# Odd-frequency transforms folded to half their matmuls, attention operands split and stacked at another time, and modulation rows transposed, in a two-block kernel

## The chip, the cores and the metric

One NeuronCore of a Trainium2 chip runs the whole program. The metric is device time in microseconds (us), the median of the runs of a kernel. The engines are named as in the profile: PE (TensorE, with PEld for its weight loads), DVE (VectorE), ACT (ScalarE), POOL (GpSimd) and SP (SyncE, which here only issues DMAs). Each runs its own instructions in order, and they wait for each other on semaphores.

## The reference

Two transformer-like blocks run one after the other on 512 tokens of width 1024, in float32. The change touches the first block only, in its mixing part:

```
hl = rmsnorm(xl, norm1_g) * (1.0 + sc1_l) + sh1_l          # sc, sh: rows of silu(c) @ ada_w + ada_b
aq, ak, av, bq, bk, bv, pool, hy = split_cols(hl @ w_in)   # and the same of 256 context tokens
a_l = diff_attention(...)            # 4 heads x 2 maps, 768 keys, softmax, p0 - lam * p1, @ v
b_l = neighbourhood_attention(...)
p_l = pool_mix(pool, ...)
h_l = hyena_mix(hy, ...)

def bidir_long_conv(u, h_fwd, h_bwd, d_skip):              # called twice by hyena_mix
    k = concatenate([h_fwd, zeros_like(h_fwd[:1]), h_bwd[:0:-1]])
    y = irfft(rfft(u, n=2 * L) * rfft(k), n=2 * L)[:L]     # L = 512
    return y + u * d_skip

z = x1 * bidir_long_conv(v, filt[:, 0, 0], filt[:, 0, 1], d_skip[0])
h = x2 * bidir_long_conv(z, filt[:, 1, 0], filt[:, 1, 1], d_skip[1])
xl = xl + g1_l * (concatenate([a_l, b_l, p_l, h_l]) @ w_out)
```

After it come a mixture of 16 experts, and a second block with attention, a state-space branch and gates. The filters `filt` come from a small network on 512 time steps.

## The kernel before, in words

The program is written engine by engine, each with its instructions in the order of the code; nothing reorders them. PSUM is used as four slots of two banks. A table of units (`units_of_block_one`, line 135) says in which order PE fills them and which engine, ACT or DVE, empties each; a unit reuses the slot of the unit four places earlier and waits for its release. `filled` waits until PE has filled a unit, `read` until it has been emptied. Weights come as slabs of 2 MB into a ring of three slots, issued by SP in the order of `SLABS_FIRST`.

The long convolutions are done as matmuls with cosine and sine tables at 512 odd frequencies, with the phase (2f+1) t pi/1024, in four tiles of 128 frequencies (QT = 4).

- Filter spectra, `spectra(f)`, four units of 2 x 4 matmuls (cosine and sine, four tiles of time, 512 columns for two filters of 256 channels). ACT copies each to `spec`. Two units stand ahead of the norm sums `n1`, `nf`, two after `ada(4)`.
- `transposes(o)` brings the gated input u to time-major form, ACT copies it to `hy_tm`; `forward(o, f)` (`fwd`, four units of 8 matmuls with 256 columns); DVE multiplies with the spectrum in `spectrum(o, f)` (four ops) into `hy_Y`; `inverse(o, c)` (`inv`, two units of 8 matmuls with 512 columns); DVE scales and gates the result (`gated`, `gate_out`).
- The first convolution (o = 0) runs after the projections. The second one (o = 1) is spread through the first attention ("a"), at the steps of `CONV_AT`: step 1 transposes, 3, 6, 9 and 11 forward, 15 and 16 inverse. A step i of this attention is, on PE, the transposes `t` of step i-1's probabilities, two score units of step i+1, a convolution unit where there is one, and the product with the values, `o`, of step i-1. On DVE it is `row_max`, `combine`, `row_max`, the convolution's ops, `output`.

The modulation rows, `ada(j)`, are twelve products of silu(c) with a slab of `ada_w`, in four row groups of PSUM; ACT copies the rows and `ada_tr(j)` sums the groups and brings them to columns in one go: four matmuls with the selection matrix `ada_sel` of two columns. DVE adds the bias.

Queries and keys of attention a are split in a rounded high part and a low rest (`q_hi_a`, `q_lo_a`, `k_hi_a`, `k_lo_a`). Both lie in hT, the normalised input, and so are written when the last projection (bv) has read hT. SP then stacks them four times over the partitions with 32 small DMAs (`stack`), the queries to `q_4` and the keys to `k_4` in the ring. The first scores wait for all 32. The tables for the forward transform are loaded twice to `fwd`, since preparations of the state-space part (`prep_pb`, `prep_ca`, `prep_ed` on DVE, stored by POOL) use the place in between; SP issues the second load when those stores have landed.

## Time and profile before

| what | value |
|---|---|
| runs | 1355.93, 1349.57, 1352.05 us |
| median | 1352.05 us |
| span of the profiled execution | 1354.0 us |
| instructions | 17167 |
| PE busy, weight loads | 1250.7 us (92%), 914.0 us (67%) |
| DVE, ACT, POOL busy | 843.6 (62%), 586.8 (43%), 132.3 us (10%) |
| mean granted clock of TensorE | 0.959 of full speed |

The profile is of one execution, and its times are in us from the start of the span. A row of the timeline gives start, length, engine, line of the code, operation, output and inputs, the shapes, and how many instructions were merged; brackets at the end give the engine's idle time just before it and who ended it. A float32 matmul shows as two records. Ends of matmuls are modelled, so that lengths of neighbouring groups overlap by a tenth or two.

### The profile page before, as it was taken

The numbers are of one execution on the slowest core, as the hardware profiler recorded it, in microseconds if no ns is written. First come the engines' busy times: TensorE is split into PE (matmuls) and PEld (weight loads), VectorE is DVE, ScalarE is ACT, GpSimd is POOL, SyncE is SP. The second block draws the span as 40 slices with busy tenths as digits, with TensorE's granted clock in tenths as the row PEclk, the third lists the DMA queues.
The fourth block names the chain that finished last, engine by engine and source line by source line (L and its number), as shares of the span: only waits on it lengthen the run. The fifth ranks groups of instructions, "written<-read, shape, count | busy, mean of one in ns | idle before, by whom it ended". The sixth has DMA issues, their size and how long they took to land.

```text
span 1354.0 us, 17167 instructions
## 1 busy us (share of the span) xinstructions
PE 1250.7 (92%) x6556; PEld 914.0 (67%) x6556; DVE 843.6 (62%) x1262; ACT 586.8 (43%) x777; POOL 132.3 (10%) x126
## 2 busy tenths in 40 slices
PE   6999999988889898699999999989999898989996
PEld 1444465766768776588888888658877777765774
DVE  3259878636866636678888898664227555724543
ACT  0540001214545553367877777533334343334322
POOL 2000101000015000112111212210000000000000
PEclk8999999998999999799999999999999999898998
DMA  8726546475040034489999999761344455534301
GB/s 361 294 76 263 226 182 246 163 156 124 1 179 21 1 129 186 143 315 397 411 409 399 408 405 406 284 245 62 114 140 132 149 172 151 166 116 180 125 0 62
DMA packets 52823, 270.69 MB, mean 200 GB/s; under 512 B 15031, under 2 KB 22071, under 8 KB 38040
## 3 DMA queue, kind: packets, MB, share of 16 engines
q1 hardware_dynamic: 38408, 210.04, 42.4%
q0 software_dynamic: 9744, 47.19, 9.5%
q10 hardware_dynamic: 4608, 12.58, 2.4%
q8 instruction: 43, 0.70, 0.2%
q14 instruction: 20, 0.16, 0.0%
HBM read 229.95 MB, written 36.70 MB: 197 GB/s over the span
## 4 chain that ended last, share of the span: by engine, by line
PE 77%; DVE 12%; ACT 4%; issue 3%; DMA 2%; POOL 1%; SPq 0%; DVEq 0%; ACTq 0%; POOLq 0%
PE PS L2736 27%; PE PS L3154 7%; PE PS L3155 7%; PE PS L3156 7%; PE PS L3068 3%; PE PS L3380 3%; PE PS L3381 3%; PE PS L3382 3%; PE PS L3285 2%; PE PS L3286 2%; PE PS L3287 2%; PE PS L3022 1%; PE PS L3366 1%; PE PS L2753 1%; PE PS L3148 1%
## 5 line engine op out<-in xcount | busy, mean ns | idle before, releaser
L2736 PE MATMUL PS<-arena 128*128 128x64 f32 (+6 forms) x770 | 188.0, 410 | 24.2 <-DMA arena<-in_small_f_w 7.7
L1385 ACT ACTIVATE arena_r<-ring 128x2048 fp32r<-128x2048 f32 x100 | 185.8, 1910 | 10.4 <-ACT arena L1422 8.1
L2736 PEld LDWEIGHTS PS<-arena 128*128 128x128 f32 (+2 forms) x770 | 114.8, 197 | 89.4 <-issue 58.4
L2186 DVE TENSOR_TENSOR arena_r<-ring,arena_r 128x2048 fp32r<-128x2048 f32 x66 | 148.1, 2285 | 20.9 <-ACT arena_r L1385 20.8
L2736 PE MATMUL PS<-hT,ring 128*128 128x512 f32 (+1 forms) x304 | 119.2, 550 | 0.0
L3154 PE MATMUL PS<-arena_r,hT_r 128*128 128x512 f32 x272 | 112.7, 414 | 4.9 <-DVE hT_r L2369 4.9
L3380 PE MATMUL PS<-arena_r 128*128 128x512 f32 x256 | 105.7, 413 | 12.0 <-DVE ring_r L2595 6.9
L3155 PE MATMUL PS<-arena_r,hT_r 128*128 128x512 f32 x272 | 109.0, 401 | 0.0
L1200 ACT ACTIVATE arena<-PS 128x1024 f32<-128x1024 f32 (+2 forms) x31 | 28.5, 926 | 169.6 <-PE PS L2736 155.0
L3382 PE MATMUL PS<-arena_r,ring_r 128*128 128x512 f32 x256 | 101.8, 398 | 0.0
L2736 PEld LDWEIGHTS PS<-hT,ring 128*128 128x128 f32 x304 | 57.1, 190 | 59.0 <-issue 56.6
L2186 DVE TENSOR_TENSOR hT_r<-ring,arena_r 128x2048 fp32r<-128x2048 f32 x34 | 76.4, 2288 | 26.6 <-ACT arena_r L1385 26.3
L2595 DVE TENSOR_TENSOR ring_r<-ring,arena_r 128x1024 fp32r<-128x1024 f32 (+1 forms) x40 | 40.4, 1011 | 69.8 <-ACT arena_r L1542 69.2
L3381 PE MATMUL PS<-hT_r,arena_r 128*128 128x512 f32 x192 | 76.6, 399 | 0.0
L1875 DVE TENSOR_TENSOR arena<-arena 128x512 f32<-128x512 f32 (+2 forms) x104 | 71.9, 691 | 3.6
L3380 PEld LDWEIGHTS PS<-arena_r 128*128 128x128 f32 x256 | 49.4, 193 | 29.6 <-issue 7.5
L3154 PEld LDWEIGHTS PS<-arena_r,hT_r 128*128 128x128 f32 x272 | 52.1, 191 | 20.4 <-DVE hT_r L2369 5.5
L3155 PEld LDWEIGHTS PS<-arena_r,hT_r 128*128 128x128 f32 x272 | 52.4, 193 | 11.1
L2410 DVE TENSOR_TENSOR ring_r<-ring,arena_r 128x1024 fp32r<-128x1024 f32 x18 | 21.9, 1224 | 59.7 <-ACT arena_r L1482 59.7
L1542 ACT ACTIVATE arena_r<-ring 128x1024 fp32r<-128x1024 f32 (+1 forms) x40 | 35.4, 885 | 53.8 <-PE PS L3382 51.0
L3382 PEld LDWEIGHTS PS<-arena_r,ring_r 128*128 128x128 f32 x256 | 49.6, 194 | 11.8
L3156 PE MATMUL PS<-arena_r,hT_r 128*128 128x512 f32 x136 | 55.4, 407 | 0.0
(473 smaller groups left out, 2388.4 us busy)
## 6 DMA issues: line engine op xcount, KB each, us to landing
ring<-in_moe SPq DMA_DIRECT2D x51, 2048.0 KB, 10.3
ring<-in_slabs SPq DMA_DIRECT2D x27, 2048.0 KB, 11.2
ring<-in_slabs SPq DMA_DIRECT2D x9, 1024.0 KB, 5.7
y_rows<-arena ACTq DMA_DIRECT2D x16, 512.0 KB, 10.0
ssm_scratch<-arena POOLq DMA_DIRECT2D x4, 1152.0 KB, 6.6
arena<-ssm_scratch POOLq DMA_DIRECT2D x4, 1152.0 KB, 8.3
arena<-in_tab_fwd SPq DMA_DIRECT2D x2, 2048.0 KB, 15.6
ssm_scratch<-arena POOLq DMA_DIRECT2D x4, 1024.0 KB, 11.6
```

Source lines behind the costliest of these rows:

```text
L1385: nc.scalar.activation(rounded(moe_w_hi[n][:, cols]), ring[:, n, cols], ACT.Copy).then_inc(s_moe_hi[n], 1)
L1875: then(nc.vector.tensor_tensor(out, x, y, op))
L2186: nc.vector.tensor_tensor(rounded(moe_w_lo[n][:, cols]), ring[:, n, cols], as_float(moe_w_hi[n][:, cols]), ALU.subtract).then_inc(s_moe_lo ...
L2595: nc.vector.tensor_tensor(rounded(w), w, as_float(w_hi[:, n % 2, 0:w.shape[1]]), ALU.subtract).then_inc(s_w_lo, 1)
L2736: ins = nc.tensor.matmul(out, lhsT, rhs, start=(n == 0), stop=(n == len(pairs) - 1))
L3068: ins = nc.tensor.matmul(bank(key, c), rounded(w[:, k]), rounded(x[:, k]), start=(m == 0), stop=(m == 3 * KD - 1))
L3154: nc.tensor.matmul(out, rounded(x_hi), rounded(w_hi_), start=first, stop=False)
L3155: nc.tensor.matmul(out, rounded(x_lo), rounded(w_hi_), start=False, stop=False)
L3156: return nc.tensor.matmul(out, rounded(x_hi), rounded(w_lo_), start=False, stop=last)
L3380: nc.tensor.matmul(out, w_h, x_h, start=(k == 0), stop=False)
L3381: nc.tensor.matmul(out, w_h, x_l, start=False, stop=False)
L3382: ins = nc.tensor.matmul(out, w_l, x_h, start=False, stop=(k == last))
```

## The change

The cosine and the sine of frequency 511 - f differ from those of f only by a sign at the even or the odd time steps. So the changed kernel sorts time into even and odd steps (`evens_odds`, `split_time`, `time_of`), computes the transforms of both halves for 256 frequencies only (FT = 2 tiles), and gets the frequencies above by a sum and a difference. The inverse does it the other way round.

- `spectra(n)`: four units of 2 x 2 matmuls (even and odd half). ACT copies the odd half (`filter_odd`), DVE forms sum and difference (`filter_spectrum`).
- `forward(o, f)`: two units of 8 matmuls with 256 columns. ACT copies the odd half (`forward_odd`). DVE: `spectrum_products` (sum, difference, two products of 1024 elements) and `spectrum_sums` (two sums, and the sum and difference for the inverse). `CONV_AT` is now {1, 4, 8, 15}; in attention a the sums run one step after the products.
- `inverse(o, c)`: two units of 8 matmuls with 256 columns.
- The short convolutions read every second element and write sorted.
- The query's and key's high and low parts have places in the arena. The query is split before `ada(11)`, ahead of the short convolutions on DVE; the key after them. SP stacks the queries when bk_ctx is filled, the keys after `ada(11)`; the second unit of bv stands between forward and inverse. DVE's sums wait for the stacked high parts of the keys, ACT's odd copy for the stacked queries, since these are overwritten. `w_in` slab 2 is laid out so that its first half is free earlier, and the ring slots 1 and 2 of the `w_in` slabs are swapped.
- The second load of `fwd`, now 1 MB, is issued by ACT.
- `ada_tr(j)`: four transposes against the identity; DVE sums the four groups with a reduce and adds the bias in an op of its own.

```diff
-SECOND_CONV = [("u_tr", 1)] + [("fwd", 1, f) for f in range(QT)] + [("inv", 1, c) for c in range(2)]
-CONV_AT = {1: 0, 3: 1, 6: 2, 9: 3, 11: 4, 15: 5}
+FT = 2
+HALF = T // 2
+SECOND_CONV = [("u_tr", 1)] + [("fwd", 1, f) for f in range(FT)] + [("inv", 1, c) for c in range(2)]
+CONV_AT = {1: 0, 4: 1, 8: 2, 15: 3}
...
+            def forward_odd(o, f):
+
+                filled(act, ("fwd", o, f))
+                if o or f:
+
+                    act.wait_ge(s_spec, FT * o + f)
+                nc.scalar.activation(hy_V[:, 1].rearrange("p a b -> p (a b)"), bank(("fwd", o, f), 1), ACT.Copy).then_inc(s_odd, 1)
...
             act.wait_ge(s_out_pb, 32 * Q_SSM)
+            act.wait_ge(s_out_ed, 32 * Q_SSM)
+            act.dma_start(fwd, tab_d["fwd"]).then_inc(s_fwd_in, 16)
+            read(act, ("ak_ctx",))
+            nc.scalar.activation(rounded(k_hi_a), k_a, ACT.Copy).then_inc(s_qk_hi, 1)
             copy_unit(("bv", 0), v_b[:, 0:4].rearrange("p a b -> p (a b)"), both(("bv", 0)))
...
+            act.wait_ge(s_stack_q, 16 * 16)
+            for f in range(FT):
+                forward_odd(0, f)
...
-                nc.vector.tensor_tensor(mod[:, a:b], bank(key, 0)[:, 0:8].rearrange("p (a b) -> p a b", b=2),
-                                        V("ada_b", a, b)[:, :, None].broadcast_to([P, b - a, 2]),
-                                        ALU.add).then_inc(s_dve_read, 1)
+                of_groups = bank(key, 0).rearrange("p (m g r) -> p m r g", m=4, g=4)[:, :, 0:2]
+                nc.vector.tensor_reduce(mod[:, a:b], of_groups, AX_X, ALU.add).then_inc(s_dve_read, 1)
+                read(dve, key)
+                then(nc.vector.tensor_tensor(mod[:, a:b], mod[:, a:b], V("ada_b", a, b)[:, :, None].broadcast_to([P, b - a, 2]),
+                                             ALU.add))
...
-            def spectrum(o, f):
+            def spectrum_products(o, f):
...
+                dve.wait_ge(s_odd, 2 * FT + FT * o + f + 1)
+                then(nc.vector.tensor_tensor(flat[:, 0], bank(key, 0), flat[:, 1], ALU.add))
+                nc.vector.tensor_tensor(flat[:, 1], bank(key, 0), flat[:, 1], ALU.subtract).then_inc(s_dve_read, 1)
...
+                then(nc.vector.tensor_tensor(hy_M, hy_V, cos_f, ALU.mult))
+                then(nc.vector.tensor_tensor(hy_V, hy_V, sin_f, ALU.mult))
+
+            def spectrum_sums(o, f):
+
+                nc.vector.tensor_tensor(hy_M[:, :, 0], hy_M[:, :, 0], hy_V[:, :, 1], ALU.subtract).then_inc(s_dve, 1)
...
+                then(nc.vector.tensor_tensor(hy_M[:, :, 1], hy_M[:, :, 1], hy_V[:, :, 0], ALU.add))
+                if o == f == 0:
+                    dve.wait_ge(s_stack_k[0], 16 * 8)
+                elif f == 0:
+                    dve.wait_ge(s_stack_k[1], 16 * 8)
+                then(nc.vector.tensor_tensor(hy_Y[o][:, f, 0], hy_M[:, 0], hy_M[:, 1], ALU.add))
+                nc.vector.tensor_tensor(hy_Y[o][:, f, 1], hy_M[:, 0], hy_M[:, 1], ALU.subtract).then_inc(s_spec, 1)
...
-                    ins = products(bank(key, 0)[:, 2 * m:2 * m + 2], [(ada_row[:, P * m:P * m + P], ada_sel[:])])
+                    ins = nc.tensor.transpose(bank(key, 0)[:, P * m:P * m + P], ada_row[:, P * m:P * m + P], ident[:])
...
             transposes(0)
-            for f in range(QT):
+            for f in range(FT):
                 forward(0, f)
+            tokens("bv", w_bv, 0, [1])
             pe.wait_ge(s_inv_in, 16)
             for c in range(2):
                 inverse(0, c)
```

How the instructions move, at three places. First PE, from the last projections to the end of the first convolution. `ring,hT ... x32` and `x16` are bv's two units, `ident,arena 128x128 x8` the transposes of u, `arena 128x256` forward or (now) inverse, `arena 128x512` the inverse before. Before:

```order
L2736 MATMUL PS<-ring,hT 128x256 x32
L2736 MATMUL PS<-ada_sel,post 128x2 x4
L2736 MATMUL PS<-ring,hT 128x256 x16
L2938 MATMUL PS<-ident,arena 128x128 x8
L2736 MATMUL PS<-arena 128x256 x32
L2736 MATMUL PS<-arena 128x512 x16
```

Now:

```order
L2772 MATMUL PS<-ring,hT 128x256 x32
L2798 MATMUL PS<-ident,post 128x128 x4
L2973 MATMUL PS<-ident,arena 128x128 x8
L2772 MATMUL PS<-arena 128x256 x16
L2772 MATMUL PS<-ring,hT 128x256 x16
L2772 MATMUL PS<-arena 128x256 x16
```

The second bv unit has moved from before the transposes to between forward and inverse, and both transforms have half their columns.

Second, DVE in a step of attention a with a forward unit: `TENSOR_REDUCE stat` is `row_max`, the op on `hT` is `combine`, `TENSOR_SCALAR arena<-PS,stat` is `output`. Before:

```order
L2066 TENSOR_REDUCE stat<-PS 128x1
L2012 TENSOR_TENSOR arena<-PS,arena 128x512
L2014 TENSOR_TENSOR rstd<-PS,arena 128x512
L2017 TENSOR_TENSOR arena<-arena,rstd 128x256
L2018 TENSOR_TENSOR arena<-arena,rstd 128x256
L2084 TENSOR_SCALAR arena<-PS,stat 128x64
```

Now, from step 4 into step 5:

```order
L2040 TENSOR_TENSOR arena<-PS,arena 128x512
L2041 TENSOR_TENSOR arena<-PS,arena 128x512
L2044 TENSOR_TENSOR arena<-arena 128x1024
L2045 TENSOR_TENSOR arena<-arena 128x1024
L2117 TENSOR_SCALAR arena<-PS,stat 128x64
...
L2117 TENSOR_SCALAR arena<-PS,stat 128x64
L2049 TENSOR_TENSOR arena<-arena 128x2x256
L2051 TENSOR_TENSOR arena<-arena 128x2x256
L2056 TENSOR_TENSOR arena<-arena 128x512
L2057 TENSOR_TENSOR arena<-arena 128x512
```

The four ops of a unit have become eight, four in its own step before `output` and four in the next one after it. There are two such units instead of four. In the first convolution the eight ops stand in a row.

Third, ACT between the last modulation row and the first scores. `arena_r` outputs are the high parts. Now:

```order
L1239 ACTIVATE arena_r<-arena 128x1024
L1141 ACTIVATE post<-PS 128x512
L1244 ACTIVATE arena<-arena,vec 128x512 x6
L1248 DMA arena<-in_tab_fwd 128x2048
L1250 ACTIVATE arena_r<-arena 128x1536
L1203 ACTIVATE arena<-PS 128x1024 x2
L1170 ACTIVATE arena<-PS 128x512 x2
L1203 ACTIVATE arena<-PS 128x512
```

Before, the query's high part stood behind both bv copies, the key's behind the copy of the transposes, the two odd copies of line 1170 and the DMA did not exist here.

## Rows read from the trace of the kernel before

**Rows 1.** The page: busy time per engine, and the chain's shares by engine.
```profile
PE 1250.7 (92%) x6556; PEld 914.0 (67%) x6556; DVE 843.6 (62%) x1262; ACT 586.8 (43%) x777; POOL 132.3 (10%) x126
...
PE 77%; DVE 12%; ACT 4%; issue 3%; DMA 2%; POOL 1%; SPq 0%; DVEq 0%; ACTq 0%; POOLq 0%
```

**Rows 2.** Timeline of PE: filter spectra (two groups) and one modulation transpose.
```profile
44.91 15.68 PE L2736 MATMUL PS<-arena 128*128 128x512 f32 x32
...
71.53 14.00 PE L2736 MATMUL PS<-arena 128*128 128x512 f32 x32
85.36 0.95 PE L2736 MATMUL PS<-ada_sel,post 128*128 128x2 f32 x8
```

**Rows 3.** Timeline of ACT in the first stage: table load after squares, root, third spectrum.
```profile
54.27 1.28 ACT L1176 ACT_TABLE_LOAD   x1
...
66.58 0.27 ACT L1185 ACTIVATE root<-PS,of_rows 128x6 f32<-128x6 f32 x1 [0.46 <-PE PS L2736]
...
78.70 1.02 ACT L1165 ACTIVATE arena<-PS 128x1024 f32<-128x1024 f32 x1 [6.44 <-PE PS L2736]
```

**Rows 4.** Timeline of DVE: tenth modulation row, and the last short convolution.
```profile
244.73 0.17 DVE L1730 TENSOR_TENSOR mod<-PS,vec 128x8 f32<-128x8 f32 x1 [3.76 <-PE PS L2736]
...
263.00 0.75 DVE L1997 SCALAR_TENSOR_TENSOR arena<-arena,vec 128x512 f32<-128x512 f32 x1
```

**Rows 5.** Timeline of PE: transposes, forward, inverse, first scores.
```profile
275.21 1.04 PE L2938 MATMUL PS<-ident,arena 128*128 128x128 f32 x8
277.96 14.05 PE L2736 MATMUL PS<-arena 128*128 128x256 f32 x64 [1.72 <-ACT arena L1200]
294.47 15.67 PE L2736 MATMUL PS<-arena 128*128 128x512 f32 x32 [2.46 <-DVE arena L2018]
309.58 2.09 PE L2736 MATMUL PS<-ring_r 128*128 128x512 f32 x8
```

**Rows 6.** Timeline of ACT (a copy of 512), DVE (1024 from SBUF, 512 from PSUM).
```profile
275.41 0.60 ACT L1200 ACTIVATE arena<-PS 128x512 f32<-128x512 f32 x1 [6.72 <-PE PS L2736]
...
276.98 1.23 DVE L2042 TENSOR_TENSOR hT_r<-arena,hT_r 128x1024 fp32r<-128x1024 f32 x1 [8.42 <-ACT hT_r L1247]
...
281.69 0.69 DVE L2012 TENSOR_TENSOR arena<-PS,arena 128x512 f32<-128x512 f32 x1 [0.67 <-PE PS L2736]
```

**Rows 7.** Stacking DMAs; median landing of the 2 MB table; a window while stacking.
```profile
L808 SPq DMA_DIRECT2D ring_r<-hT_r x32: 594/602/1547, 277.0 to 300.9; - x32
...
arena<-in_tab_fwd SPq DMA_DIRECT2D x1, 2048.0 KB, 8.7
...
282.00:290.00 8.00, 8.00 (x39) 7.04 (x38) 5.26 (x11) 0.00 (x0) 0.00 (x0) 1.00 0.96 205
```

**Rows 8.** Timeline of PE and DVE in attention a, steps 3 to 16.
```profile
326.54 0.85 PE L3022 MATMUL PS<-ident,hT 128*128 128x128 f32 x6 [0.31 <-DVE hT L2076]
...
333.53 0.82 PE L3022 MATMUL PS<-ident,hT 128*128 128x128 f32 x6
...
336.08 1.02 DVE L2076 SCALAR_TENSOR_TENSOR hT<-hT,stat 128x768 f32<-128x768 f32 x1
...
337.24 0.85 PE L3022 MATMUL PS<-ident,hT 128*128 128x128 f32 x6 [0.37 <-DVE hT L2076]
...
341.19 0.82 PE L3022 MATMUL PS<-ident,hT 128*128 128x128 f32 x6
...
377.01 0.84 PE L3022 MATMUL PS<-ident,hT 128*128 128x128 f32 x6 [0.44 <-DVE hT L2076]
...
386.71 8.32 PE L2736 MATMUL PS<-arena 128*128 128x512 f32 x28
...
399.60 7.13 PE L2736 MATMUL PS<-arena 128*128 128x512 f32 x16
```

**Rows 9.** Windows (us): length, busy PE, PEld, DVE, ACT, POOL, clock, DMA share, GB/s.
```profile
294.00:298.00 4.00, 3.53 (x5) 1.57 (x6) 0.72 (x2) 0.00 (x0) 0.00 (x0) 0.63 1.04 224
...
345.00:360.00 15.00, 13.10 (x86) 11.22 (x85) 12.54 (x23) 8.03 (x15) 0.00 (x0) 1.00 0.00 1
```

More of the change, by code:

```diff
@@ L2948, in forward @@
                     pe.wait_ge(s_fwd_in, 32)
-                for cs in range(2):
-                    products(bank(key, 0)[:, HY * cs:HY * cs + HY],
-                             [(fwd[:, cs, t, P * f:P * f + P], hy_tm[:, t]) for t in range(QT)], last=(cs == 1))
+                for odd in range(2):
+                    for cs in range(2):
+                        products(bank(key, odd)[:, HY * cs:HY * cs + HY],
+                                 [(fwd[:, cs, t, P * f:P * f + P], hy_tm[:, t]) for t in range(2 * odd, 2 * odd + 2)],
+                                 last=(odd == cs == 1))
             def inverse(o, c):
@@ L2955, in inverse @@
                 start_unit(key)
-                pe.wait_ge(s_spec, QT * (o + 1))
-                products(bank(key, 0), [(hy_Y[:, f, cs, P * c:P * c + P], inv[:, cs, f])
-                                        for cs in range(2) for f in range(QT)], last=True)
+                pe.wait_ge(s_spec, FT * (o + 1))
+                for odd in range(2):
+                    times_ = slice(HALF * odd, HALF * odd + HALF)
+                    products(bank(key, 0)[:, times_], [(hy_Y[o][:, f, odd, cs, P * c:P * c + P], inv[:, cs, f, times_])
+                                                       for cs in range(2) for f in range(FT)], last=(odd == 1))
             def second_conv(n):
@@ L2966, in _ @@
             transposes(0)
-            for f in range(QT):
+            for f in range(FT):
                 forward(0, f)
+            tokens("bv", w_bv, 0, [1])
             pe.wait_ge(s_inv_in, 16)
@@ L3535, in slabs_of @@
         elif name == "w_in":
-            out.append(k_major(a["w_in"][0][:, 512 * j:512 * j + 512], 512))
+            w, cols = a["w_in"][0][:, 512 * j:512 * j + 512], 256 if j == 2 else 512
+            out.append(np.concatenate([k_major(w[:, at_:at_ + cols], cols) for at_ in range(0, 512, cols)], axis=1))
         elif name == "w_out":
```

202 lines of the change are left out of this document (102 added, 100 removed).

## The prediction

> **What bounds the kernel now.** I read the page's busy shares first: TensorE (PE) is busy 92% of the span, VectorE (DVE) 62%, ScalarE (ACT) 43%, and the chain of work that ended last lies 77% on PE, 12% on DVE [rows 1]. So PE's matmuls set the time, except where PE waits. Then I read PE's timeline over the first 400 us, since the change ends there. In it the reader should see long groups without idle brackets (every matmul removed there is time gained, as long as nothing else comes last), and a few groups with brackets, which name who comes last. Four places matter: the filter transforms at 44.91 and 71.53 [rows 2], the first convolution at 277.96 to 309.58 [rows 5], the first attention at 326.54 to 377.01 [rows 8], and the inverse transforms at 386.71 and 399.60 [rows 8].
>
> A float32 matmul shows as two records, and its time goes by columns: 32 records of 512 columns take 14.00 us (0.44 each) [rows 2], 64 of 256 take 14.05 (0.22 each) [rows 5]. A transpose is one record: six take 0.82 [rows 8].
>
> **First stage, -15.0 us.** The filter spectra fall from 32 to 16 matmuls of 512 columns, 14.0 us less on PE. Half of them stand ahead of the norm sums. There ACT ends its squares at 54.27 and computes the norm's root at 66.58 [rows 3]; between, it waits for PE. After the change PE's first spectra end near 52.8 (44.91, less 0.9 for the faster row transposes ahead, plus half of 15.68 and the 0.9 us that the slow clock costs beyond that half), so ACT comes last: table load 1.28 and a short root 0.1, two copies of 0.5 (the new odd halves, which are 512 wide), a copy of 0.8, and PE's small matmuls until the root, 1.6. From 53.9 (squares 0.4 earlier) that gives the root at 58.7, 7.8 us earlier. The second pair saves its full 7.0 [rows 2]: the normalised h is ready in time, since ACT's copy of the third spectrum, for which it waited 6.44 us ahead of h [rows 3], now stands behind h. Each of the modulation transposes saves about 0.4: eight records of 2 columns take 0.95 [rows 2], four transposes at 0.11 each take 0.5. One of them lies here: 7.8 + 7.0 + 0.4, less 0.2 for rounding, 15.0. What comes next late here would be a slab for PE; the DMA engines are idle most of the time from 56 on and the forward table is 1 MB less, so I cost loads at nothing.
>
> **From there to the first transform, -2.6 and -7.1.** Seven more row transposes (5 to 11) lie before it: 7 x 0.37 = 2.6. The second bv product, 32 records of 256 columns or 7.1 us by the price above, moves behind the forward transforms. PE would so reach the transposes of u at 275.2 - 15.0 - 2.6 - 7.1 = 250.6. Is DVE ready? It is the engine with most to do here. Its preparation chain starts after two more sums per filter spectrum (4 x 1.35 us), 14.1 us earlier than before; but it waits for PE twice on the way, last at 244.73 for 3.76 us [rows 4], and that wait ties it to PE again: -17.0 there, -16.8 after the extra op. Then 9.0 for the last preparation, the query low part now ahead of the convolution (1.23, [rows 6]), and 8.8 for twelve short convolutions, the last of which starts at 263.00 [rows 4]. It is done at 246.9, 3.7 us before PE. These twelve now read every second element. The bound above is twice their time, 8.8 us more, of which 5.1 would reach PE; below it is nothing, as the op's form stays. I take nothing. The modulation's extra reduce and add (0.25 us, 12 times) is in those figures.
>
> **First convolution, -5.2.** Before, from the transposes at 275.21 to the scores at 309.58: 34.4 us. After, step by step from 250.6. Transposes and ACT's copy 2.4: PE starts forward at 253.0. One forward unit still has 8 matmuls of 256, 3.45 us, but there are two. DVE sees it 0.2 later, at 256.7, and first ACT copies the odd half (0.6, as the 0.60 row of [rows 6]). Then DVE has eight ops where it had four [rows 6]: two on PSUM at 0.69, two products of 1024 elements at 1.23, and four of 512 at 0.69, with 0.04 between, 6.7 us where it was 2.2. ACT's second odd copy waits until all that is done, as it overwrites an operand, so the second unit runs wholly behind: 256.7 + 2 x (0.65 + 6.75) = 271.5. PE has its second forward unit and bv (to 267.2) as cover and then idles 4.3 us. Then the inverses, half the columns: 7.0, plus 1.7 for the slow clock after an idle stretch, which the same place shows now (15.68 for a 14.0 group [rows 5], clock 0.63 [rows 9]). End 280.3, scores 0.6 earlier as before, 279.7: 29.1 us, bv among them. Sum so far: 15.0 + 2.6 + 7.1 + 5.2 = **-29.9**.
>
> **The copies between.** The stacking of queries and keys takes 32 transfers of 128 or 192 KB, 5.2 MB, at 205 GB/s while the DMA engines are 0.96 busy [rows 7]. They had ended well before the scores. Now SP waits for the query split (236) and the bk_ctx products, and queued behind that wait stand only these copies. Sum of DMA work ahead of the key high copies' end, one after the other: queries 2.1 MB 10.5 us, prep stores 4, forward table 1 MB at half of 8.7 us [rows 7], key high 1.6 MB 7.9. From 236.1 that is 262.9; DVE needs them at its seventh op, about 262.5. I put +0.4. The low copies end near 271, wanted first at 280. ACT, which now issues the forward load, waits for the prep stores until at most 245; behind it in its queue is the bv copy, for which PE is ready at 250.4 only.
>
> From the trace alone the copies load the engines to 0.96. The Trainium skill, page "Trainium Kernel Development and Optimization", section Key Constraints, says that DMAs of the SP, ACT and POOL queues run on the same 16 engines and interleave, so the new queue buys only issue time. By that rule the forward table, issued at 245 beside the copies, may land at 255 and not at 250, and the sum would be +2 where a free queue would leave it at nothing; no row yet shows both at once.
>
> **First attention, +3.2.** Here a step without a convolution unit takes 3.95 us (337.24 to 341.19), one with a forward unit 6.99 (326.54 to 333.53), and ten steps with four units 50.5 (to 377.01) [rows 8]: a unit costs 2.9 over a base of 3.9, since PE sets such a step and DVE's 2.2 us hide in it. The change drops two units, and the tempting sum is -5.8. But DVE itself has 3.5 of the 3.9 us to do (a combination of 1.02 [rows 8], two row maxima of nearly as much, small ones), and a unit now brings it 6.7 us: 4.0 in its own step, 2.8 in the next. I follow it: t=0 at the step's transposes, unit filled at 5.9, odd copy to 6.6, products to 10.5, output, maximum and combination to 13.0, next transposes at 13.1 (now 10.7); the sums then hold the following ones to 19.3 (now 14.7); the step behind is 3.7. Four steps 22.9 where the base has 15.6: 7.3 per unit, 14.7 for two, against 11.5 for four now.
>
> **Inverses of the second convolution, -7.0.** PE sets both: the groups at 386.71 (with twelve small records) and at 399.60 have no idle ahead of what follows [rows 8], and each loses half of 7.0. What comes next in the second, the exponential's table load and DVE's maxima, also moves up.
>
> Sum: -29.9 + 0.4 + 3.2 - 7.0 = **-33.3**. Nothing later changes, and the expert stage, where DMA is full, starts earlier as a whole. The profiled execution has a span of 1354.0, so 1320.7; the median of the runs shown is 1352.05, 2 us less, and I forecast 1352.05 - 33.3 = 1319.
>
> **Rivals.**
> 1. DVE's extra work hides in attention as it does now: 2 units at 2.9, so 8.9 better, 1310. For it: the units stand four steps apart. Against: DVE has 0.4 us free per step.
> 2. PE's clock. Its idle stretches grow (4.3 us before the inverses, about 2 us in attention beside the waits for DVE). A gap of 2.5 us sufficed for 0.63 of the clock at 294 to 298, while from 345 to 360, with gaps below 1 us, it is 1.00 [rows 9]. Each fall costs 1.7 us where PE decides; two to five of them: 1322 to 1328.
> 3. Copies or table late: the interleaving above, +2 to +6: 1321 to 1325.
> 4. The first stage gives half, because a slab load or h comes last after all: 1326.
> 5. Slower than before: attention falls to the half clock and stays there, since its PE work (0.8 of transposes, 1.2 of scores and 1.5 of values) then takes 6 to 6.5 us and each step some 2.3 more; 16 steps, 37 us, for 1356. It decides from the point where the loss passes 33 us, which needs nearly all steps. Against it: 1.00 throughout the waits of now.
> 6. The change does not halve: the count in the order and the equal price per column exclude it but for 1%.
>
> **Chances.** Forecast (1315 to 1322) 0.50; rival 1 0.13; rival 2 0.16; rival 3 0.11; rival 4 0.06; rival 5 0.02; the last 0.02 for the sixth and what I don't see. Leaving out 0.2 at the most, the range is 1309 to 1327. A difference within 0.5%, 6.8 us, can't be told from no change here: faster 0.96, same 0.02, slower 0.02.
>
> **What would show it.** Pool products at about 71 on PE, not 86; transposes of u near 251 and not waiting for DVE; 4 us idle on PE before the inverse, released by DVE; transposes of attention 6 us apart twice after each unit; scores of the first attention at 280. Wrong would be: PE waiting for the stacked copies, steps of 3.9 behind a unit, or a first stage that moves by less than 12 us.

## The result, and the profile after

The changed kernel takes 1332.05 us (median of four runs, 1328.5 to 1342.4); the runs of the kernel before beside it give a ratio of 0.9847 (95% interval 0.9812 to 0.9883). Measured once more it is 1339.58 us and 0.9896 (0.9845 to 0.9946). So it is faster, by 16 to 20 us between the medians. I had forecast 1319, with a range from 1309 to 1327: the sign is right and the size is not.

The page of the profiled execution, with a span of 1332.2 us (before 1354.0): busy times, and the chain by engine.

```profile
PE 1220.0 (92%) x6412; PEld 899.1 (67%) x6412; DVE 862.2 (65%) x1282; ACT 588.6 (44%) x781; POOL 129.2 (10%) x126
...
PE 74%; DVE 13%; ACT 5%; DMA 3%; issue 3%; SPq 2%; POOL 1%; DVEq 0%; ACTq 0%; POOLq 0%
```

Against [rows 1] PE has 31 us less to do and DVE 19 more, and the chain has moved a little from PE to DVE. The span is only 22 us shorter. Where the rest went is read from PE's timeline. These are the groups that answer to [rows 2] and [rows 5], then the row of DVE that the prediction named as a danger:

```profile
45.79 7.03 PE L2772 MATMUL PS<-arena 128*128 128x512 f32 x16
...
62.80 2.91 PE L2772 MATMUL PS<-arena,ones 128*128 128x512 f32 x4
65.64 3.38 PE L2789 MATMUL PS<-ring,arena 128*32 128x512 f32 x16
68.94 7.13 PE L2772 MATMUL PS<-arena 128*128 128x512 f32 x16
75.92 0.60 PE L2798 MATMUL PS<-ident,post 128*128 128x128 f32 x4
76.35 6.17 PE L2893 MATMUL PS<-hT,ring 128*128 128x512 f32 x14
...
255.43 1.04 PE L2973 MATMUL PS<-ident,arena 128*128 128x128 f32 x8
257.69 7.14 PE L2772 MATMUL PS<-arena 128*128 128x256 f32 x32 [1.22 <-ACT arena L1203]
277.07 8.71 PE L2772 MATMUL PS<-arena 128*128 128x256 f32 x32 [5.33 <-DVE arena L2057]
285.43 1.88 PE L2772 MATMUL PS<-ring_r 128*128 128x512 f32 x8
```

```profile
268.00 0.69 DVE L2056 TENSOR_TENSOR arena<-arena 128x512 f32<-128x512 f32 x1 [0.53 <-DMA ring_r<-arena_r]
```

The counted work came out: both spectra groups are 7.0, a row transpose 0.60, the forward group 7.1, PE stands 5.3 us ahead of the inverse and is released by DVE. The two groups between them (62.80 and 65.64) are the diagonal sums and `ada(4)`; they took 1.53 and 1.92 us before, with the same work. In attention a (`t` groups of steps 4 to 8 and 10 to 12, which answer to [rows 8]):

```profile
305.81 0.82 PE L3064 MATMUL PS<-ident,hT 128*128 128x128 f32 x6
...
312.58 0.83 PE L3064 MATMUL PS<-ident,hT 128*128 128x128 f32 x6
...
318.84 1.51 PE L3064 MATMUL PS<-ident,hT 128*128 128x128 f32 x6 [0.66 <-DVE hT L2109]
...
324.80 1.51 PE L3064 MATMUL PS<-ident,hT 128*128 128x128 f32 x6 [0.57 <-DVE hT L2109]
...
329.48 0.85 PE L3064 MATMUL PS<-ident,hT 128*128 128x128 f32 x6 [0.26 <-DVE hT L2109]
...
342.74 1.51 PE L3064 MATMUL PS<-ident,hT 128*128 128x128 f32 x6 [0.66 <-DVE hT L2109]
...
348.70 1.51 PE L3064 MATMUL PS<-ident,hT 128*128 128x128 f32 x6 [0.58 <-DVE hT L2109]
...
355.03 1.25 PE L3064 MATMUL PS<-ident,hT 128*128 128x128 f32 x6 [1.27 <-DVE hT L2109]
```

Six transposes take 0.82 to 0.85 us, but 1.51 in steps 6 and 7 and in steps 10 and 11, where the units stand in steps 4 and 8. The windows say why: length, busy PE, PEld, DVE, ACT, POOL, then the granted clock. Steps 3 to 13, after and before:

```profile
301.80:359.50 57.70, 46.76 (x253) 40.06 (x253) 47.70 (x77) 28.88 (x53) 2.35 (x1) 0.79 0.09 33
```

```profile
326.50:377.00 50.50, 44.05 (x284) 37.98 (x285) 41.51 (x77) 27.75 (x51) 3.00 (x1) 1.00 0.04 9
```

There are 31 fewer matmul records, and PE is busy 2.7 us longer, since TensorE was granted 0.79 of its clock on average (at times the lower of its two levels, 1.2 GHz, where before it had the upper one, 2.4 GHz, throughout).

### The profile page after: what moved, and what is told of

Its sections match the earlier page's. It is cut to its first block, busy times and chain, and to the rows that moved or that the text cites. A ratio compares the mean times of both kernels' runs of the same rounds, so it can differ in the third digit from the quotient of the medians.

```text
span 1332.2 us, 16908 instructions
## 1 busy us (share of the span) xinstructions
PE 1220.0 (92%) x6412; PEld 899.1 (67%) x6412; DVE 862.2 (65%) x1282; ACT 588.6 (44%) x781; POOL 129.2 (10%) x126
## 4 chain that ended last, share of the span: by engine, by line
PE 74%; DVE 13%; ACT 5%; DMA 3%; issue 3%; SPq 2%; POOL 1%; DVEq 0%; ACTq 0%; POOLq 0%
PE PS L2772 21%; PE PS L3196 7%; PE PS L3197 7%; PE PS L3198 7%; PE PS L3110 3%; PE PS L3422 3%; PE PS L3423 3%; PE PS L3424 3%; PE PS L3328 2%; PE PS L3327 2%; PE PS L3329 2%; PE PS L3064 2%; PE PS L3408 1%; SPq L804 1%; PE PS L2789 1%
## 5 line engine op out<-in xcount | busy, mean ns | idle before, releaser
L2772 PE MATMUL PS<-arena 128*128 128x64 f32 (+6 forms) x674 | 150.1, 390 | 30.0 <-DMA arena<-in_small_f_w 7.6
L2772 PEld LDWEIGHTS PS<-arena 128*128 128x128 f32 (+2 forms) x674 | 100.2, 205 | 73.9 <-issue 40.5
L2223 DVE TENSOR_TENSOR hT_r<-ring,arena_r 128x2048 fp32r<-128x2048 f32 x34 | 76.4, 2288 | 26.9 <-ACT arena_r L1394 26.2
L3422 PEld LDWEIGHTS PS<-arena_r 128*128 128x128 f32 x256 | 49.2, 192 | 30.9 <-issue 9.7
L3424 PEld LDWEIGHTS PS<-arena_r,ring_r 128*128 128x128 f32 x256 | 49.2, 192 | 11.6
## 6 DMA issues: line engine op xcount, KB each, us to landing
ssm_scratch<-arena POOLq DMA_DIRECT2D x4, 1024.0 KB, 10.9
```

Source lines behind the costliest of these rows:

```text
L2223: nc.vector.tensor_tensor(rounded(moe_w_lo[n][:, cols]), ring[:, n, cols], as_float(moe_w_hi[n][:, cols]), ALU.subtract).then_inc(s_moe_lo ...
L2772: ins = nc.tensor.matmul(out, lhsT, rhs, start=(n == 0), stop=(n == len(pairs) - 1))
L3422: nc.tensor.matmul(out, w_h, x_h, start=(k == 0), stop=False)
L3424: ins = nc.tensor.matmul(out, w_l, x_h, start=False, stop=(k == last))
```

## The experiments

Each starts from the changed kernel, unless it says otherwise. To compare stages rather than medians I use distances on PE's timeline: first filter spectrum to pool products ("first stage"), pool products to transposes of u, from there to the scores ("convolution"), the t groups of steps 3 and 13 ("ten steps"), and step 13 to the first t of attention b ("the end"). In the first traces they were, before, 41.3, 189.04, 34.4, 50.5 and 29.6; after 30.6, 179.08, 30.0, 57.7 and 22.7.

**Both kernels once more.**

> The changed kernel once more, untouched, for a second trace. If the half-clock spells are a property of the program (my theory), they stand at the same places again: 62 to 69 behind the norm sums (ada(4) near 3.4 us, n1d near 2.9), behind both forward units of the first attention (transposes of 1.5 us instead of 0.85), and steps of 6.8, 6.3, 6.0, 4.7 and 7.0, 6.3, 6.0, 6.3. If they are chance (rival), at least one place reads 1.00 with ada(4) at 1.9. The spells near 424 and 444 in the second attention and at the third filter layer (1.7 us) I take as open: this trace tells whether they recur. Time 1332, ratio to the kernel before 0.985.

> The kernel before once more, untouched, for a second trace of it. Three traces of the new form show a mean granted clock of 0.83 to 0.86 from 300 to 375 (before: 0.96 over the first attention). If the spells come with the change, this trace again shows the clock near 1.00 between the third step and the inverses, and the ten steps with four units take 50.5 us. If they are chance, it shows half-clock transposes (1.5 us) there too, and ten steps of 52 or more. Open, since the runs of the new form differ in it: the third filter layer takes 7.1, 11.8 or 14.0 us; here it took 12.3 and I can't say which it will be. Time 1352 to 1356.

The changed kernel: first stage 30.1 with the diagonal sums at 2.91 and `ada(4)` at 3.44, pool products to u 179.08 again, convolution 29.6, steps of 6.77, 6.26, 5.96, 4.67 and 7.00, 6.26, 5.96, 6.34, 5.18. The first eight are those of the first trace to 0.02 us; the last, step 12, took 4.49 there. The kernel before (1354.42 us, ratio 0.9973, 0.9943 to 1.0004): 41.3, 189.04, 34.4, 50.5, and a granted clock of 1.00 over the ten steps. So the spells (stretches at the lower clock) in the first stage and behind the units come with the change. Not all do. The end took 27.6 in this trace of the changed kernel and 22.7 in the first, and 31.7 against 29.6 before; from the first t of attention b to the end of the span it was 947.4 and 948.9 before, 950.0 and 951.7 after, and 948.2 on average over twelve kernels below that change nothing there (940.7 to 953.8). The spells near 424 and 444 of the first trace belong to that scatter.

The third filter layer (`f3`) is a lottery of its own. It took 7.13 us here and 14.02 in the first trace, for the same sixteen records:

```profile
20.48 7.13 PE L2772 MATMUL PS<-arena 64*128 64x512 f32 x16 [0.72 <-ACT arena L1146]
```

```profile
20.24 14.02 PE L2772 MATMUL PS<-arena 64*128 64x512 f32 x16 [0.72 <-ACT arena L1146]
```

Both traces show a granted clock of 1.00 from 20 to 36 us, though the group of 14.02 us runs at half the pace. Up to 4 of the 7 us are left when the first spectrum starts (41.8 against 45.8; before 44.9 twice).

**The first stage.** PE's norm sums wait for ACT's squares after the change. Two kernels filled that wait. The first moves the third filter spectrum (PE's part is shown; ACT's and DVE's moved likewise):

```diff
             spectra(0)
             spectra(1)
+            spectra(2)
...
             ada(4)
-            spectra(2)
             spectra(3)
```

> The changed kernel with the third filter spectrum moved ahead of the norm sums, on PE, ACT and DVE. PE then has 3.5 us of dense products while ACT finishes its squares, and the norm sums run in one piece as they did before the change. Clock theory: no half clock between 62 and 69, n1d 1.5 and ada(4) 1.9 us, pool products start at 71.5 instead of 76.35, so 5 us less (3.3 of clock, 1.7 of waiting for squares), time near 1327. Rival (the squares and DVE's new sums alone set the stage, the clock is chance): the root comes 1.5 to 3.5 later, the spell stays, and pool products start between 75 and 77, no change in time.

The second adds four products of 128x512 in a bank that nobody reads:

```diff
+            banks_free(pe, ("nf",))
             for k in range(KD):
+                if k >= 4:
+                    nc.tensor.matmul(bank(("nf",), 1), ident[:], even_odd[:, 0, 0].rearrange("p a b -> p (a b)"), start=True, stop=True)
                 pe.wait_ge(s_sq, 2 * k + 2)
```

> The changed kernel with four products of 512 columns that nobody reads, one ahead of each of the last four waits for ACT's squares in the norm sums; PE does 1.75 us more work there, in time that it waits. Clock theory: n1d 1.5 and ada(4) 1.9 us, pool products start at 73 to 74 instead of 76.35, though PE does more. Rival (no clock effect, or the work that matters is elsewhere): pool products at 76.3 to 78, n1d and ada(4) slow as before.

With the third spectrum ahead the spell was gone in this trace, as expected, and the gain was not 5 but 1.9 us (first stage 28.7; median 1335.59, ratio 0.9851, 0.9772 to 0.9930, no different from the changed kernel):

```profile
62.11 1.53 PE L2772 MATMUL PS<-arena,ones 128*128 128x512 f32 x4
63.57 1.92 PE L2789 MATMUL PS<-ring,arena 128*32 128x512 f32 x16
...
72.35 4.96 PE L2893 MATMUL PS<-hT,ring 128*128 128x512 f32 x11 [2.79 <-issue]
```

The pool products now stand four units behind the diagonal sums and so reuse their PSUM slot, which DVE holds until h is scaled; PE waited 2.79 us for it. I had counted work and not slots. The filling products failed: first stage 35.5 us, 5 longer (median 1338.82, ratio 0.9892, 0.9857 to 0.9927). The rows explain the length. Eight norm sums (128x32 tiles) take 1.08 us when they stand together and two of them take 1.05 beside a full-width product, so these tiles run side by side only with one another:

```profile
52.82 1.08 PE L2850 MATMUL PS<-arena,ones 128*32 128x512 f32 x8
...
54.27 1.12 PE L2847 MATMUL PS<-arena,ident 128*128 128x512 f32 x2
55.32 1.05 PE L2850 MATMUL PS<-arena,ones 128*32 128x512 f32 x2
```

The spell came all the same: PE did not wait between the first spectrum and the diagonal sums, and these took 2.91 again, with a granted clock of 1.00 up to 68 us and 0.50 from 70 to 72. So the waits for the squares are not needed for the spell in this stage, and the clock theory of this run failed.

**Attention a: who holds a step.** The query of attention b was split in step 11, its high part on ACT, its low part on POOL. In the trace of the changed kernel a DVE op on one column took 1.88 us beside that POOL op, 0.22 elsewhere:

```profile
351.47 2.35 POOL L1002 TENSOR_TENSOR hT_r<-arena,hT_r 128x1024 fp32r<-128x1024 f32 x1 [108.19 <-ACT hT_r L1304]
351.77 0.15 DVE L2106 RECIPROCAL stat<-stat 128x2 f32<-128x2 f32 x1
351.96 1.88 DVE L2107 SCALAR_TENSOR_TENSOR stat<-stat,lam 128x1 f32<-128x1 f32 x1
```

```diff
             nc.scalar.activation(lam[:, 2:4], lam[:, 0:2], ACT.Exp).then_inc(s_lam_e, 1)
+            act.wait_ge(s_spec, FT)
+            read(act, ("bk_ctx",))
+            nc.scalar.activation(rounded(q_hi_b), q_b.rearrange("p j (i c) -> p j i c", c=256),
+                                 ACT.Copy).then_inc(s_qk_hi, 1)
...
-                if i == 9:
```

> The changed kernel with one edit: the query of the second attention is split at the start of the first inverse transform, where ACT and DVE are idle, and no longer at step 10 of the first attention. Theory: the 1.88 us for a DVE op on one column beside POOL's low part (0.22 elsewhere) is DVE held until POOL ends, so it goes, and so do ACT's 1.04 ahead of the copy of the transposes: the step that took 6.33 takes about 4.2, time 2 us less, near 1330. Rival (the long op has another cause, the step is slow by the half clock): a step of 5.9 or more stays and the time with it. A second check: POOL's op in its new place lies beside DVE at rest and costs nothing there; scores stay near 285.4.

The step fell from 6.33 to 5.18 (the transposes behind it still at 1.49), the ten steps from 57.7 to 55.7, and the median was 1327.01 (ratio 0.9807, 0.9745 to 0.9868). The direction is as expected, but the step is not at 4.2, since the half clock stayed. Nor is all of the 2.0 the query's: 0.7 of it lies in step 7, which took 3.95 and not 4.68 because the clock was up again earlier, long before the place of the query's op.

**How much of it is the clock.** Score products that nobody reads fill PE's waits: first only the last two lines of the diff, in steps 5 and 9, then all of it, on top of the early query split.

> The changed kernel with eight score products that nobody reads ahead of the value products in steps 5 and 9, where PE waits 2.2 us for DVE's output: PE is busy there and does 2 us more work. Clock theory: the transposes after that wait take 0.85 and not 1.5 us in steps 6, 7, 10 and 11, the steps behind become 4.0 instead of 4.7, and step 4 to step 12 takes 46.5 to 48 us instead of 49.2. Rival (DVE alone sets these steps; the half clock hides behind it): step 4 to step 12 at 49.2 or more, whatever the clock does.

```diff
+            def fill(key, times):
+                for _ in range(times):
+                    nc.tensor.matmul(bank(key, 1), rounded(q_4[:, 0, 0:P]), rounded(k_4[:, 0, 0:T]), start=True, stop=True)
...
+                        if a == "a" and i in (5, 6, 9, 10, 12, 13):
+                            fill(("a", "o", i - 1), {5: 3, 6: 7, 9: 3, 10: 7}.get(i, 3))
...
+                        if a == "a" and i in (4, 8):
+                            fill(("a", "o", i), 8)
```

> The kernel with the early query split, and score products that nobody reads wherever PE waits for DVE in the first attention: eight ahead of the value products of steps 5 and 9, three to seven ahead of the transposes of steps 6, 7, 10, 11, 13 and 14. Clock theory: with no gaps PE keeps the full clock, all transposes take 0.85 us, and from step 3 to step 13 the time is what the prediction gave without any fall, 53.7 us (55.7 in the run with the early query split alone, 57.7 in the changed kernel), and from there to the second attention 22.7 instead of 25.0. So 3 to 4 us less than that run. Rival (the half clock hides behind DVE all along): 55 to 56 and 25 stay.

With steps 5 and 9 alone filled (1330.23 us, 0.9816, 0.9788 to 0.9843), steps 4 to 12 took 49.2 as before. The transposes of step 6 were back at 0.85 us and the steps took 6.26 and 5.96 as ever; the half clock came one step later and the fourth step was 4.68. There the rival was right: steps 5 and 6 are DVE's, at either clock. It is the steps after them that the clock lengthens. With all waits filled and the query moved (1332.03, 0.9846, 0.9804 to 0.9889), steps 3 to 13 took 3.96, 6.75, 6.17, 5.96, 4.04, 6.70, 6.18, 5.96, 4.04 and 4.40, 54.2 in all, where the prediction had 53.7 (the median does not show it: it is 5 us above that of `q_split_early`, with intervals that overlap):

```profile
301.60:355.80 54.20, 47.87 (x293) 38.47 (x293) 46.67 (x78) 27.91 (x52) 0.00 (x0) 1.00 0.10 35
```

The 3.5 us between 57.7 and 54.2 divide so. In steps 3 to 10, ahead of the query's op, 1.1 went, which is the clock's. Steps 11 and 12 took 10.8 together in the changed kernel, 9.8 with the query moved and 8.4 with the waits filled too. So the clock has about 2.5 and the query's split about 1.0, when they are taken away in this order. But the end was 24.6 and not 22.7. In step 13 POOL's other low part started 0.04 us ahead of the combination:

```profile
358.28 3.50 POOL L1005 TENSOR_TENSOR arena_r<-arena,arena_r 128x1536 fp32r<-128x1536 f32 x1 [78.10 <-ACT arena_r L1308]
358.32 4.28 DVE L2109 SCALAR_TENSOR_TENSOR hT<-hT,stat 128x768 f32<-128x768 f32 x1
```

**Whether POOL holds DVE.** The edit: `pool.wait_ge(s_prob, n)` ahead of that POOL op, so that it starts behind the combination of step 13.

> Four edits together: the third filter spectrum ahead of the norm sums with the pool products ahead of the fifth row transposes; the early query split; the products that nobody reads in PE's waits of the first attention; and POOL's low part of the second attention's keys starts only when DVE's combination of step 13 is done. In the run with the fills, POOL started 0.04 us ahead of that combination and DVE's op took 4.28 us instead of 1.02. Theory (a DVE op that reads two tensors from SBUF waits until POOL is done): the combination takes 1.02 again, POOL is through before the next one, step 13 takes 5.3 instead of 6.9, and from step 13 to the second attention 23 instead of 24.6. Pool products 27 us behind the first spectrum, steps 3 to 13 at 54.2. Time 1320 to 1325, ratio 0.977. Rival (the long op has another cause): step 13 or 14 still takes 6 to 7.

The count of 13 was one too low (step 13's combination is the fourteenth), so the wait did nothing: POOL started 0.04 us ahead of the op once more, which took 4.27, and step 13 took 6.85. As a test of the cause this run is void; as a time it gave 1331.55 (0.9809, 0.9790 to 0.9827). With a count of 14 and nothing else changed against `fill_more`:

> The kernel with the early query split and the filling products, and one edit more: POOL's low part of the keys waits for the fourteenth combination, that of step 13 (with a count of thirteen it had not waited at all). Theory (a DVE op that reads two tensors from SBUF stands until POOL's op is done): POOL starts when the combination ends, the combination takes 1.02 and not 4.28 us, the step from the thirteenth to the fourteenth transposes takes 5.3 instead of 6.86, unless the next op with two inputs comes while POOL still works (3.5 us), which would then hold step 14. From step 13 to the second attention 22.5 to 23.1 instead of 24.6. Rival (the long op has another cause): 6.8 and 24.6 stay.

```profile
353.79 1.02 DVE L2110 SCALAR_TENSOR_TENSOR hT<-hT,stat 128x768 f32<-128x768 f32 x1
...
354.95 3.51 POOL L1006 TENSOR_TENSOR arena_r<-arena,arena_r 128x1536 fp32r<-128x1536 f32 x1 [79.06 <-DVE hT L2110]
```

The same op takes 1.02, the step 5.38, the end 22.8 (the prediction had 22.6), and the median is 1327.19 (0.9784, 0.9757 to 0.9811). That settles it: a DVE op that reads two tensors from SBUF, started while POOL's tensor_tensor runs, stands until POOL is done. DVE's row maximum, which reads PSUM, and its reciprocal, with one input, ran beside POOL at their usual 0.95 and 0.16. The Trainium skill, page "GPSIMD Engine Reference", section Specifications, says that GpSimd shares its SBUF interfaces with VectorE and contends with instructions that have two SBUF inputs; the traces agree, with 1.66 and 3.26 us for one instruction, and the prediction had not drawn on it. Nor had it seen that the trace of the kernel before holds such a pair, at the end of the filter network; this op takes 0.67 elsewhere:

```profile
33.98 2.35 POOL L973 TENSOR_TENSOR arena<-arena 128x1024 f32<-128x1024 f32 x1 [1.07 <-DVEq L1751]
34.00 2.89 DVE L1755 TENSOR_TENSOR arena<-arena 128x512 f32<-128x512 f32 x1
```

**Where the units stand.**

> The changed kernel with the second forward unit at step 6 of the first attention and not at 8. Theory (a unit costs what DVE has left over after it, because its eight ops come at the end of the unit's own step): DVE's sums of the first unit then stand in step 5, and its catching up in step 6 lies beside PE's second unit: steps of 6.8, 6.3, 6.8, 6.3, 6.0, 4.7 and then 4.0, so 44.5 us from step 4 to step 12 instead of 49.2, time 1328 to 1331. Rival (the clock sets these steps, and two units so near each other pull it down for longer): 48 to 50 us, with transposes of 1.5 in steps 5 to 9 throughout, and no gain.

```diff
-CONV_AT = {1: 0, 4: 1, 8: 2, 15: 3}
+CONV_AT = {1: 0, 4: 1, 6: 2, 15: 3}
```

The ten steps took 56.3, 1.4 less and not 4.7; steps 4 to 12 took 48.7, within the rival's 48 to 50. The median was 1332.43 (0.9831, 0.9806 to 0.9857), no different from the changed kernel. Steps 6 and 7 took 7.41 and 7.54. DVE stood 1.62 us for the unit and its odd copy, and PE's scores then waited for the unit's PSUM slot, its value products for DVE's output behind the products:

```profile
324.45 0.59 ACT L1170 ACTIVATE arena<-PS 128x512 f32<-128x512 f32 x1
325.14 0.69 DVE L2040 TENSOR_TENSOR arena<-PS,arena 128x512 f32<-128x512 f32 x1 [1.62 <-PE PS L3064]
...
326.61 0.62 PE L2772 MATMUL PS<-ring_r 128*128 128x512 f32 x2 [1.19 <-DVE arena L2041]
...
329.45 2.52 PE L2772 MATMUL PS<-arena 128*128 128x64 f32 x12 [2.22 <-DVE arena L2117]
```

I took the odd copy's place, behind an exponential on ACT, for the cause. The next two kernels carry the third spectrum, with a new place for one modulation row so that the pool products reuse another slot, the early query split and this `CONV_AT`:

```diff
             spectra(3)
-            ada_tr(4)
...
             pair(("pool",), w, 0, first_time=True)
+            ada_tr(4)
```

> Three edits on the changed kernel: the third filter spectrum ahead of the norm sums, now with the pool products ahead of the modulation's fifth transposes (they waited 2.8 us for a PSUM slot in the run before); the query split of the second attention at the first inverse; the second forward unit at step 6. Theory: 4.5 us in the first stage (pool products 26 us behind the first spectrum instead of 30.5), 2.4 from the query, 4.7 from the unit, so 11 to 12 less than the changed kernel, 1321 to 1326. Rival (spells of half clock fall where the waits now stand and give part of it back): 1327 to 1332.

and on top of it, on ACT:

```diff
+                        if (a, i, c) == ("a", 7, 1):
+                            forward_odd(1, 1)
                         act.wait_ge(s_max, j + 1)
...
-                        elif key[0] == "fwd":
+                        elif key == ("fwd", 1, 0):
```

> The kernel with the three edits, and ACT's odd copy of the second unit ahead of the exponential of score 7 and no longer behind it. In the run before, DVE stood still for 1.9 us at step 6 for that copy, and step 6 and 7 took 8.95 and 6.54. Theory: the copy ends at once when the forward products end, DVE's products start 0.8 to 1.4 us earlier, PE's scores don't wait for the unit's slot, and step 3 to step 13 falls from 55.65 to 54.0 to 54.8. Rival: the copy now holds the exponential, which the combination waits for, and nothing is won (55.5 or more).

`three_edits`: 1328.05 (0.9796, 0.9771 to 0.9820), where its rival had it and not the theory, first stage 26.9, ten steps 55.65, the two steps 8.95 and 6.54. With the odd copy first: 1325.79 (0.9792, 0.9754 to 0.9830), ten steps 55.6, the two steps 8.94 and 6.53. The copy's place on ACT changed nothing, because in both traces PE's forward products themselves were slow (6.50 us where 4.90 is usual); placed first, the copy only waited 2.39 us for them. My theory of the odd copy fell; the neighbouring units cost about what they cost apart.

**One part undone, and the clean version.**

```diff
-                    ins = nc.tensor.transpose(bank(key, 0)[:, P * m:P * m + P], ada_row[:, P * m:P * m + P], ident[:])
+                    ins = products(bank(key, 0)[:, 2 * m:2 * m + 2], [(ada_row[:, P * m:P * m + P], ada_sel[:])])
```

> One part of the change undone: the modulation's row sums again by four products with two columns, and DVE's one op instead of two. By the prediction's price of 0.37 to 0.4 us each, seven of them stand between the pool products and the transposes of u: 181.7 to 181.9 us between these two instead of 179.08, which four traces of the changed form agree on to 0.01. Rival (DVE's own chain sets that stretch, and the second op on DVE costs what PE gains): 179.1 stays.

From pool products (74.38) to transposes of u (256.42): 182.04, 2.96 more. The row transposes are worth 0.42 each. (It ran once, in 1341.56 us, which says nothing by itself.)

> Three edits without any filling products: third filter spectrum ahead of the norm sums with the pool products ahead of the row transposes, early query split, POOL's key part behind the combination of step 13. Theory: no DVE op is held by POOL; the half clock stays where PE waits (steps 6, 7, 10, 11), so steps 3 to 13 take 55.5 to 56.5 and step 13 to the second attention 22.7 to 25. Pool products 27 to 28.5 us behind the first spectrum: two of three traces with this order had the slow n1d of 2.91 us all the same, so I expect 28.5 here. Time 1322 to 1328.

This one gives 1325.84 (0.9797, 0.9776 to 0.9818), with no unread products. First stage 25.3 us, with both groups at the full clock, ten steps 55.0, the end 23.1. It is as good as `fill_wait14` within their intervals, and level with `odd_first` (0.9792), `three_edits` (0.9796) and `q_split_early` (0.9807), which have no unread products either; it lies about 0.5 to 1% below the changed kernel. But the third spectrum ahead does not secure the clock: of five traces with that order, the diagonal sums took 1.53, 1.63, 2.91, 2.91 and 1.53 us. What decides it stays open.

## Why the prediction was wrong

The sum by its own steps, as distances averaged over the two traces of each kernel (predicted, then measured). The two spans differ by 22.3 on average; the medians of the runs differ by 20.0 and 15.6, and single executions of one kernel scatter by up to 20 us, so the stages tell more than the totals.

| step | predicted | measured |
|---|---|---|
| start to first spectrum | -0.9 | -1.1 (+0.9 and -3.1) |
| first stage | -14.1 | -10.9 |
| pool products to transposes of u | -9.7 | -10.0 |
| convolution, with the copies | -4.8 | -4.6 |
| scores to step 3 | 0 | -0.5 |
| steps 3 to 13 | +3.2 | +7.5 |
| step 13 to attention b | -7.0 | -5.5 |
| the rest | 0 | +2.7 |
| sum | -33.3 | -22.4 |

1. **First stage: mis-sized by 3.2.** The order of events was right: ACT came last, the root moved from 66.58 to 60.76, 5.8 earlier, where I had 7.8. The spectra began 0.9 later than before in that trace and not 0.9 earlier, which is most of the difference; measured from the first spectrum, the root came 15.0 behind it, where I had 14.7. What I had left out is PE's clock behind the root. I costed the small matmuls, the diagonal sums and `ada(4)` at the lengths of the kernel before. The windows from 58 to 70 show a granted clock of 0.50 from 62 to 68 where it was 1.00 before. The three groups from 60.53 on took 8.7 us there and 5.4 before, 3.3 more. What brings the lower clock here is open: ahead of it PE waited for the squares, but `fill_first` shows the same spell without a wait. From the start of the span, the pool products moved 9.8 us in the first trace and 14.2 in the second; less than 12 had been named as a sign of being wrong.
2. **Row transposes and the moved bv: right.** -10.0 against -9.7, and 179.08 in seven traces. DVE finished its twelve convolutions in time, at 0.75 us each as before, although they now read every second element: the bound of 8.8 us above was not touched.
3. **First convolution: right, as a sum.** The two DVE passes began at 262.2 and 270.2, 8.0 us apart (I had 7.4); the inverse took 8.7, of which some 3 us at the lower clock (0.50 from 277 to 279, 0.69 from 279 to 281), as taken over from [rows 5]. The rival of the late copies lives here: DVE's wait for the stacked keys was 0, 0, 0, 0.41, 0.53, 0.64, 0.86 and 1.54 us in eight traces, in which the table issued by ACT landed after 7.3, 6.7, 7.8, 8.7, 8.5, 8.8, 8.7 and 9.3. In the other six it was 0 five times (6.3 to 8.0) and 1.56 once (9.7). The longer the table takes beside the copies, the later the keys. The mean over the fourteen is my +0.4. A transfer of 1 MB took as long as one of 2 MB had on its own (8.7, [rows 7]); so half of 8.7 for the table was too low. By the rule of the Trainium skill that the prediction cited (page "Trainium Kernel Development and Optimization", section Key Constraints) the queues' transfers interleave; the trace agrees.
4. **The ten steps: the step that failed.** The term is the +3.2, from "7.3 per unit"; it measured +7.5. "7.3 per unit" is what a unit costs with the clock up: steps 4 to 7 of `fill_more` are 6.75, 6.17, 5.96 and 4.04, together 22.9, and I had 22.9. What I did not see is two things that act on the steps behind. PE's waits of 2.2 us for DVE bring the half clock, and where DVE has caught up, the slower transposes and scores set the step (about 2.5 us over ten steps). I had this as a rival, at 1.7 for each fall, and gave it 0.16, on the ground that the clock was at 1.00 in the steps of before [rows 9]; but those steps had no wait above 1 us, and mine had. The second thing was no rival: the shift in time brought DVE's two-input ops under POOL's low parts. With the query's copy on ACT it cost about 1.0. In both traces of before, these two POOL ops started while DVE's combination was running and delayed no DVE op, so nothing in [rows 8] showed it; the row at 34.00, in another stage of the same trace, did.
5. **The end: right where nothing interferes.** 22.7 in the first trace and 22.8 in `fill_wait14` against 22.6; 27.6 in the second trace, where POOL held DVE for 2.3 us in step 13 and the clock was low for the following two steps.
6. **The rest, +2.7,** is scatter: the mean over twelve other kernels equals that of before.
7. **The rivals.** The clock (0.16) was the right one, and its 1322 to 1328 too narrow, since POOL was missing and so was the spell in the first stage; the copies cost 0.53 and nothing in the two traces; that all hides in attention, and that the half clock stays through all of it, was wrong; the first stage gave 10.9 of 14.1.

With the waits filled and POOL kept off, the two stretches of attention take 54.2 and 22.8, 0.7 together above the prediction's own sum. The working was sound for an engine at its full clock and for engines that don't disturb each other. The first assumption stood against a rival that had too little weight, the second was made in silence.

## What to carry to other kernels

Work taken from the bounding engine turns into waits, and a wait can have a second price, paid by the next steps through the clock, as in attention here: when a change makes gaps like these 2.2 us, cost the steps behind it at both levels, and put the sum's middle between them. When an edit shifts two engines against each other, list the POOL ops in the shifted stretch and the DVE ops with two SBUF inputs beside them; a single one, even on one column, stood 1.7 to 3.3 us here, of which 1.0 and 1.8 reached PE, and a wait that started POOL right behind such an op cost nothing. Before placing an edit into a fixed order of PSUM slots, look which unit held the slot it will take.

## What the hardware showed that I had not expected

- One DVE instruction with two SBUF inputs beside a POOL tensor_tensor: 1.88 us for one column (0.22 alone), 4.28 for 768 elements (1.02 alone). POOL's own op took 2.35 and 3.50 in those cases, and 3.0 and 3.7 in the traces of before, where it started in the last 0.8 and 0.4 us of a DVE op with two inputs: there it was POOL's op that grew.
- Two inputs are not the only case. In all sixteen traces one DVE op with a single SBUF input, a TENSOR_SCALAR of 16 elements, started just behind a POOL op of 1.26 us and took 1.23; an op of its form and size takes 0.17 elsewhere (at 382.91 in the same trace). DVE ops with one input from PSUM and one from SBUF kept their 0.70 beside POOL.

```profile
396.99 1.23 DVE L2144 TENSOR_SCALAR o_root<-o_root 128x16 f32<-128x16 f32 x1
```

- The granted clock in the records can be wrong: sixteen records took 14.02 us, half the pace, at a recorded 1.00 in four traces, 7.13 at 1.00 in three, and 12.3 at 0.57 in the trace of before. The Trainium skill, page "TensorE: Matmul & The Clock Gate", section Seeing it yourself, warns that these records have been seen to be unreliable, and this trace agrees; the length of a known group is the safer sign.
- Eight 128x32 matmul records took 1.08 us together, two took 1.05 when full-width products stood between them.
- Twelve fp32 DVE ops that read with a stride of two took 0.75 us each, the same as before without it.
